# Decoder trunk on one core: TensorE warmed ahead of x's statistics, five weight units multiplied by TensorE, and half sums taken inside chunks 7, 9, 11 and 13

## The chip, the cores and the metric

One NeuronCore of a Trainium2 chip. The metric is the device time of one execution in microseconds (us). Engines: TensorE (PE in the profile; its weight loads are PEld), VectorE (DVE), ScalarE (ACT), GpSimd (POOL), and SyncE (SP), which issues the transfers.

## What is computed

Two layers over a sequence of 256 tokens of width 2048, float32. Each layer modulates a normalised x by a vector that comes from `c`:

```
c_act = silu(c)
for l in range(2):
    mod = c_act @ ada_w[l] + ada_b[l]                  # 2048 x 6144 weights for one row
    shift, scl, gate_res = split(mod, 3)
    h = rms(x, norm_g[l]) * (1 + scl) + shift
    z = h @ w_in[l]                                    # 2048 x 6144 (even layer)
    y = mixer branches and attention of z
    x = x + gate_res * ((y * silu(g)) @ w_out[l])
```

The change is in the opening: the statistics of x, `mod` of layer 0, h of layer 0, and the first twelve column slabs of `z`.

## The kernel before, in words

Everything is held transposed: a **chunk** is 128 of the 2048 features for all 256 tokens, so x and h are 16 chunks. `ada_w` is cut in **pieces** of 1024 columns; pieces 0 to 3 give scale and shift of h's chunks 0 to 3, 4 to 7, 8 to 11 and 12 to 15. A piece is 16 **units**: unit k holds 128 rows by 1024 columns (512 KB). Units are numbered on through the pieces: 0 to 15, 16 to 31, 32 to 47, 48 to 63.

*VectorE sums the units.* `add_units` (L1224) does acc += unit x cact[:, k] on 128 x 1024. In pieces 2 and 3 a unit holds two row blocks of half of the columns, and `half_units` (L1241, L1244) adds them by two instructions of 128 x 512, with a wait between. So the first eight units of such a piece finish its first half, which is enough for two chunks of h. `ada_done` counts the units added.

*TensorE sums over the partitions.* `reduce_part` (L929) multiplies 128 columns of acc by a column of ones; four of them make half of a piece. The trace shows two passes (rows of x1) for each float32 matmul. `half_sum` and `mod_sum` tell VectorE that the halves are there; `first_half(p)` and `second_half(p)` then add the bias (L1248), make the gain (L1261) and scale two chunks of x each (`norm_x`, L1297). ScalarE adds the shift (`full_h`, L523) and rounds a copy (L526), which releases the chunk for TensorE by `h_done`.

*Twelve slabs at once.* `unsplit_chunk(c)` (L895) multiplies chunk c of h by the 12 weight tiles of that chunk, 128 x 128 by 128 x 256 in plain float32, into six banks. The 192 weight tiles come in 12 transfers of 16 tiles (1 MB each, `load_wide`, L287), numbers 0 to 11. Only after chunk 15 are the banks read (ScalarE, L653), and the kernel goes on to slab 12 and the rest.

*x's statistics.* ScalarE squares the chunks of x (L517) into two buffers in turn; TensorE sums each by `x_stat` (L908), two matmuls with a moving operand of one column. VectorE makes the root and a diagonal of it (L1274 to L1288), `spread_token` (L919) spreads it, and ScalarE copies it (L645). `keep_warm` (L825) multiplies ones by the identity, 128 columns, for no result.

*The order around the change* is written out by hand on every engine. TensorE: 16 statistics, spread; 4 warm-up matmuls behind each of units 10 to 14; both halves of piece 0's sum; chunks 0 to 3; 12 warm-up matmuls; piece 1's sums; chunks 4, 5, 6; first half of piece 2; chunks 7, 8; second half of piece 2; chunks 9, 10; first half of piece 3; chunks 11, 12, 13; second half of piece 3 (L1087 to L1089); 6 warm-up matmuls; chunks 14, 15. SyncE issues all loads in one order: units and wide tiles mixed. A ring of 12 buffers holds the units, so the load of unit n waits until unit n - 12 is added, and wide load i waits until wide load i - 4 is used. A load that waits holds up all loads behind it.

Of the kernel before, what the change touches and what calls it, by code (L numbers as in the profile page):

```python
# [54 lines left out]

UNSPLIT = WIDE[0]
RING = 12
TILES = KC

def wide_done(i):
# [45 lines left out]
def build(nc, xT, params, pool_w, w_slabs, ada_units, x1_dram, outT):  # L107
    ctx = ExitStack()
    with ctx:
# [3 lines left out]
        def sem(name):  # L113
            return ctx.enter_context(nc.semaphore(name))
# [67 lines left out]
        acc_zero = sem("acc_zero")  # L182
        mod_sum = sem("mod_sum")
        half_sum = sem("half_sum")
        mod_done = sem("mod_done")
        cexp = sem("cexp")
        const = sem("const")
# [52 lines left out]
        def unit_slot(n):  # L240

            return n % RING if n < FIRST else n % 4

# [69 lines left out]
        @block.sync  # L313
        def _(sp):
            sp.sem_inc(lo_done, 4 + 2 * UNSPLIT)
            sp.sem_inc(ada_done, 4)
            sp.dma_start(par[:], params).then_inc(par_in, 16)
            def load_units(n, count, t):
                for u in range(count):
                    unit = n + u if t is None else n + u + 4 * t  # L320
                    if n >= FIRST:
                        sp.wait_ge(ada_done, unit + 1)
                    elif unit >= RING:
                        sp.wait_ge(ada_done, unit - RING + 5)
                    sp.dma_start(unit_at(n + u), ada_units[bass.ds(unit, 1)].rearrange("a p n -> p (a n)"))\
                      .then_inc(ada_in[unit_slot(n + u)], 16)

            def load_halves(p, first, last):
                for n in range(first, last):
                    unit, half, u = UNITS * p + n, n // 8, n % 8  # L330
                    sp.wait_ge(ada_done, unit - RING + 5)
                    sp.dma_start(unit_at(unit).rearrange("p (a n) -> p a n", a=2),
                                 ada_units[UNITS * p + 2 * u:UNITS * p + 2 * u + 2, :,
                                           PIECE // 2 * half:PIECE // 2 * (half + 1)]
                                 .rearrange("a p n -> p a n")).then_inc(ada_in[unit_slot(unit)], 16)

            load_units(0, 4, None)
            for part in range(2):
                sp.dma_start(X[:, HC * part:HC * (part + 1), :], xT[:, HC * part:HC * (part + 1), :])\
                  .then_inc(x_in[part], 16)  # L340
            load_units(4, UNITS - 4, None)
            load_wide(sp, 0)
            load_units(UNITS, 3, None)
            load_wide(sp, 1)
            load_units(UNITS + 3, 4, None)
            load_wide(sp, 2)
            load_units(UNITS + 7, 9, None)
            load_wide(sp, 3)
            for i, first, last in ((4, 0, 3), (5, 3, 8), (6, 8, 11), (7, 11, 13), (8, 13, 16)):
                load_halves(2, first, last)  # L350
                load_wide(sp, i)
            for i, first, last in ((9, 0, 8), (10, 8, 12), (11, 12, 16)):
                load_units(3 * UNITS + first, last - first, None)
                load_wide(sp, i)

            def step(w, t):
                load_slab(sp, w + AHEAD, t)
                load_units(*units_at(w), t)

            for w0, w1 in ((10, 14), (14, 22), (22, 34), (34, 48), (48, 62), (62, 72),  # L360
                           (72, 91), (91, 99), (99, 110), (110, 125), (125, 131),
                           (131, 132), (132, N_SLABS - AHEAD)):
                if w0 in (10, 34, 48, 62, 110, 131):
                    for w in range(w0, w1):
                        step(w, None)
                else:
                    run(sp, w0, w1, step)

            for j in range(KC - 4, KC):
                w = O1 + j  # L370
                sp.wait_ge(z_free[w % 2], w // 2 + 2)
                sp.dma_start(outT[:, j:j + 1, :], X[:, j:j + 1, :]).then_inc(last_store, 16)
            sp.wait_ge(last_store, 4 * 16)
# [443 lines left out]
        def _(pe):  # L817
# [67 lines left out]
                    if k == 7:  # L885
                        last.then_inc(pe_half, 1)

            def unsplit_chunk(c):

                pe.wait_ge(h_done, c + 1)  # L890
                for s in range(WIDE[0]):
                    i, k = (WIDE[0] * c + s) // TILES, (WIDE[0] * c + s) % TILES
                    if s == 0 or k == 0:
                        pe.wait_ge(wide_in[i % 4], 16 * (i // 4 + 1))
                    last = mm(wide(s), wide_tiles(i)[:, k, :], X[:, c, :], start=(c == 0 and s % 2 == 0),  # L895
                              stop=(c == KC - 1), skip_group_check=True)
                    if k % 8 == 7:
                        last.then_inc(pe_half, 1)
# [13 lines left out]
            def x_stat(i, runtime=None):  # L912
                pe.wait_ge(sq_done, (i if runtime is None else runtime) + 1)
                by_token(M, T[:, i % 2, :], i % KC == 0, i % KC == KC - 1).then_inc(stat_done, 1)
# [132 lines left out]

            pe.wait_ge(const, 3)
            for i in range(KC):  # L1050
                x_stat(i)
            spread_token(0)

            def warm_until(units, last):
                for u in range(units, last + 1):
                    pe.wait_ge(ada_done, u + 4)
                    keep_warm(4, O[:, SEQ:SEQ + P])

            halved = (2, 3)  # L1060

            def reduce_half(p, half):
                pe.wait_ge(ada_done, UNITS * p + 8 * (half + 1) + 4 if p in halved else UNITS * (p + 1) + 4)
                if not half and p:
                    pe.wait_ge(mod_done, p)
                for j in range(4 * half, 4 * half + 4):
                    ins = reduce_part(p, j, half=True)
                if not half:
                    ins.then_inc(half_sum, 1)

            for c in range(12):
                p = c // GROUP
                if c % GROUP == 0 and p not in halved:
                    if p:
                        warm_until(UNITS + 13, UNITS + 15)
                    else:
                        warm_until(11, 15)
                    reduce_half(p, 0)
                    reduce_half(p, 1)
                if c % GROUP == GROUP - 1 and p + 1 in halved:  # L1080
                    reduce_half(p + 1, 0)
                if c % GROUP == 1 and p in halved:
                    reduce_half(p, 1)
                unsplit_chunk(c)
            unsplit_chunk(12)
            unsplit_chunk(13)
            pe.wait_ge(ada_done, UNITS * 4 + 4)  # L1087
            for j in range(4, HC):
                reduce_part(3, j)  # L1089
            keep_warm(6, M[:, 0:P])  # L1090
            unsplit_chunk(14)
            unsplit_chunk(15)

# [106 lines left out]
        def _(dve):  # L1200
# [16 lines left out]
            def add_units(first, count, t):  # L1217
                for u in range(count):
                    unit = first + u if t is None else first + u + 4 * t
                    p = first // UNITS  # L1220
                    k = unit - UNITS * p
                    dve.wait_ge(ada_in[unit_slot(first + u)], 16 * unit_uses(first + u, t))
                    dve.wait_ge(ada_done, unit + 4)
                    dve.scalar_tensor_tensor(acc[:, p % 2, :], unit_at(first + u), cact[:, bass.ds(k, 1)],  # L1224
                                             acc[:, p % 2, :], ALU.mult, ALU.add).then_inc(ada_done, 1)

# [242 lines left out]
                norm_x(0, GROUP * p + 3)  # L1469

            dve.wait_ge(acc_zero, 1)
            add_units(0, 11, None)
            dve.wait_ge(stat_done, KC)
            rsqrt(0, QT, M[:, 0:QT], D_MODEL)
            token_diag()
            add_units(11, 5, None)
            dve.wait_ge(r_copied, 1)
            first_half(0)
            second_half(0)
            dve.wait_ge(acc_zero, 2)  # L1480
            add_units(UNITS, 16, None)
            dve.wait_ge(acc_zero, 3)
            first_half(1)
            second_half(1)
            half_units(2 * UNITS, 8)
            half_units(2 * UNITS + 8, 1)
            first_half(2)
            half_units(2 * UNITS + 9, 7)
            dve.wait_ge(acc_zero, 4)
            half_units(48, 1)  # L1490
            second_half(2)
            half_units(49, 7)
            half_units(56, 1)
            for j in range(6):
                lower_h(0, j)
            first_half(3)
            half_units(57, 7)
            second_half(3)
            for j in range(6, 14):
                lower_h(0, j)  # L1500
            lower_h(0, 14)
            lower_h(0, 15)

            def plain(w, t):
# [305 lines left out]
```

## Time and profile before

| | us |
|---|---|
| median of 3 runs | 976.7 (976.35 to 978.91) |
| the profiled execution, its own time | 974.86 |
| its span in the profile | 973.1 |
| TensorE busy | 943.4 (97%) |
| VectorE busy | 821.9 (84%) |
| ScalarE busy | 422.2 (43%) |

The profiled execution is 1.84 us under the median. "Busy" is the time in which an engine ran an instruction; the chain is followed back from the last instruction of the program to what released each step. All times of the trace are from the start of the span.

### The profile page before, as it was taken

How to read it: one execution, taken by the hardware profiler on the slowest of the kernel's cores; microseconds unless marked ns; L12 is line 12 of the kernel's file. 1: busy time of each engine (PE TensorE's matmuls, PEld its weight loads, DVE VectorE, ACT ScalarE, POOL GpSimd, SP SyncE). 2: the span in 40 equal slices, each digit the busy share in tenths (PEclk: the TensorE clock that was granted, in tenths of full speed). 3: DMA queues.
4: the chain of work that ended last, by engine and by line, in shares of the span. 5: the costliest groups of instructions: out<-in, count | busy, mean ns of one | idle time of the engine just before them, and what ended most of it. 6: DMA issues, size and time to landing. Idle time of an engine off the chain costs nothing.

```text
span 973.1 us, 18608 instructions
## 1 busy us (share of the span) xinstructions
PE 943.4 (97%) x7082; PEld 909.2 (93%) x7082; DVE 821.9 (84%) x1260; ACT 422.2 (43%) x726; POOL 65.1 (7%) x76
## 2 busy tenths in 40 slices
PE   4899999999999999999999999999999999999998
PEld 4887889999998999999999999999999989998887
DVE  5888979978998888998787999888999986879963
ACT  3110135445655444344444544444556555743331
POOL 1000000010110000222100000000011100000000
PEclk9999999999999999999999999999999999999999
DMA  9999988998876879899758555544455545688962
GB/s 366 412 403 403 413 320 277 323 348 326 327 266 242 314 262 337 326 364 355 284 198 319 179 190 180 178 143 151 153 184 185 175 168 199 201 313 295 358 224 78
DMA packets 76084, 261.28 MB, mean 269 GB/s; under 512 B 7776, under 2 KB 8416, under 8 KB 74096
## 3 DMA queue, kind: packets, MB, share of 16 engines
q1 hardware_dynamic: 73680, 251.38, 72.2%
q0 software_dynamic: 2336, 8.98, 2.5%
q8 instruction: 44, 0.72, 0.3%
q14 instruction: 24, 0.20, 0.1%
HBM read 256.07 MB, written 4.19 MB: 267 GB/s over the span
## 4 chain that ended last, share of the span: by engine, by line
PE 73%; DVE 18%; DMA 3%; issue 2%; ACT 2%; SPq 0%; DVEq 0%; ACTq 0%
PE bank L838 13%; PE bank L839 13%; PE bank L840 13%; PE bank L859 6%; DVE wlo L1214 6%; PE bank L895 5%; PE bank L982 4%; PE bank L984 4%; PE bank L985 4%; PE bank L857 3%; DMA ada<-ada_units 3%; DVE Y L1441 3%; DVE acc L1224 2%; PE bank L908 2%; DVE acc L1244 1%
## 5 line engine op out<-in xcount | busy, mean ns | idle before, releaser
L505 ACT ACTIVATE whi<-raw 128x1024 fp32r<-128x1024 f32 x258 | 272.1, 1060 | 384.5 <-PE bank L840 214.2
L1214 DVE TENSOR_TENSOR wlo<-raw,whi 128x1024 fp32r<-128x1024 f32 x258 | 312.6, 1227 | 71.9 <-ACT whi L505 70.7
L838 PE MATMUL bank<-hhi,whi 128*128 128x256 f32 x912 | 262.5, 288 | 3.1 <-DVE wlo L1214 1.4
L839 PE MATMUL bank<-hlo,whi 128*128 128x256 f32 x912 | 258.0, 283 | 0.0
L840 PE MATMUL bank<-hhi,wlo 128*128 128x256 f32 x912 | 257.9, 283 | 0.0
L1224 DVE SCALAR_TENSOR_TENSOR acc<-ada,cact,acc 128x1024 f32<-128x1024 f32 x140 | 183.0, 1307 | 22.9 <-DMA ada<-ada_units 12.6
L838 PEld LDWEIGHTS bank<-hhi,whi 128*128 128x128 f32 x912 | 174.8, 192 | 5.9 <-issue 3.1
L839 PEld LDWEIGHTS bank<-hlo,whi 128*128 128x128 f32 x912 | 174.9, 192 | 0.1
L840 PEld LDWEIGHTS bank<-hhi,wlo 128*128 128x128 f32 x912 | 174.8, 192 | 0.0
L982 PE MATMUL bank<-whi,hhi 128*128 128x256 f32 x512 | 146.7, 286 | 0.0
L984 PE MATMUL bank<-whi,hlo 128*128 128x256 f32 x512 | 144.8, 283 | 0.0
L985 PE MATMUL bank<-wlo,hhi 128*128 128x256 f32 x512 | 144.8, 283 | 0.0
L982 PEld LDWEIGHTS bank<-whi,hhi 128*128 128x128 f32 x512 | 98.2, 192 | 0.8 <-issue 0.7
L1441 DVE SCALAR_TENSOR_TENSOR Y<-U,par,Y 128x256 f32<-128x256 f32 x240 | 98.6, 479 | 0.0
L984 PEld LDWEIGHTS bank<-whi,hlo 128*128 128x128 f32 x512 | 98.2, 192 | 0.1
L985 PEld LDWEIGHTS bank<-wlo,hhi 128*128 128x128 f32 x512 | 98.2, 192 | 0.0
L859 PE MATMUL bank<-both_g,whi 128*128 128x512 f32 x256 | 89.7, 398 | 0.0
L838 PE MATMUL bank<-both_g,whi 128*128 128x256 f32 x256 | 73.2, 286 | 0.3 <-DVE both_g L1335 0.3
L839 PE MATMUL bank<-both_g,whi 128*128 128x256 f32 x256 | 72.4, 283 | 0.0
L840 PE MATMUL bank<-both_g,wlo 128*128 128x256 f32 x256 | 72.4, 283 | 0.0
L857 PE MATMUL bank<-both_g,wlo 128*128 128x256 f32 x240 | 68.1, 284 | 0.0
L859 PEld LDWEIGHTS bank<-both_g,whi 128*128 128x128 f32 x256 | 47.3, 188 | 10.4 <-DVE X L1350 0.2
(194 smaller groups left out, 1276.5 us busy)
## 6 DMA issues: line engine op xcount, KB each, us to landing
raw<-w_slabs SPq DMA_DIRECT2D x258, 512.0 KB, 4.6
ada<-ada_units SPq DMA_DIRECT2D x152, 512.0 KB, 6.6
pre<-ada_units SPq DMA_DIRECT2D x40, 512.0 KB, 15.5
raw<-w_slabs SPq DMA_DIRECT2D x6, 1024.0 KB, 15.9
V<-w_slabs SPq DMA_DIRECT2D x3, 1024.0 KB, 14.8
Y<-w_slabs SPq DMA_DIRECT2D x3, 1024.0 KB, 15.9
X<-xT SPq DMA_DIRECT2D x2, 1024.0 KB, 9.7
x_dram<-X POOLq DMA_DIRECT2D x4, 512.0 KB, 8.2
```

The source lines that it names most:

```text
L505: act.activation(whi[:, slot], raw[:, slot], ACT.Copy).then_inc(hi_done, 1)
L838: mm(out, whi[:, s, k, :], ahi[:, c, :], start=(c == 0), stop=False)
L839: mm(out, whi[:, s, k, :], alo[:, c, :], start=False, stop=False)
L840: last = mm(out, wlo[:, s, k, :], ahi[:, c, :], start=False, stop=(c == KC - 1))
L857: mm(out[:, 0:SEQ], wlo[:, s, k, :], ghi[:, c, :], start=False, stop=False, skip_group_check=True)
L859: last = mm(out[:], whi[:, s, k, :], flat(both_g[:, c]), start=(c == 0), stop=(c == KC - 1), skip_group_check=True)
L982: mm(out, hhi[:, c, tokens], upper, start=(c == 0 and q == 0), stop=False, skip_group_check=True)
L984: mm(out, hlo[:, c, tokens], upper, start=False, stop=False, skip_group_check=True)
L985: last = mm(out, hhi[:, c, tokens], lower, start=False, stop=(c == KC - 1), skip_group_check=True)
L1214: dve.tensor_tensor(wlo[:, s], raw[:, s], whi[:, s].bitcast(F32), ALU.subtract)\
L1224: dve.scalar_tensor_tensor(acc[:, p % 2, :], unit_at(first + u), cact[:, bass.ds(k, 1)], acc[:, p % 2, :], ALU.mult, ALU.add).then_inc(ada ...
L1441: ins = dve.scalar_tensor_tensor(Y[:, j, :], U[:, j, k:k + SEQ], par[:, wcol:wcol + 1], Y[:, j, :], ALU.mult, ALU.add)
```

## The change

1. TensorE starts with 30 warm-up matmuls, ahead of the statistics, and does 8 more between the statistics and the spread. The warm-ups behind units 10 to 14, ahead of piece 1's sum and behind the last half sum are gone; 3 stand behind the sums of pieces 0 and 1, after the first scaled chunk.
2. Units 9, 11, 13, 15 and 31 are multiplied by TensorE itself (`add_unit`): eight matmuls each with the unit as weights and one column of `cact` as moving operand, into the same banks as the sums. VectorE adds the other 27 of pieces 0 and 1. Piece 0's and 1's sums are taken by `reduce_whole`, which adds to what `add_unit` left. VectorE makes the statistics' root behind its first 8 units instead of behind 11.
3. The half sums of pieces 2 and 3 stand inside chunks 7, 9, 11 (ahead of the eighth tile) and 13 (ahead of the tenth). On VectorE `first_half(2)` comes two units later, and the six `lower_h` ahead of `first_half(3)` go to the end.
4. SyncE waits for `pe_added` where the buffer was used by one of the five units.

```diff
+ON_PE = (9, 11, 13, 15, 31)
+def added(unit):
+    return unit if unit >= UNITS else sum(u not in ON_PE for u in range(unit))
...
+            def slot_free(unit):
+                last = unit - RING
+                if last in ON_PE:
+                    sp.wait_ge(pe_added, ON_PE.index(last) + 1)
+                elif last >= 0:
+                    sp.wait_ge(ada_done, added(last) + 5)
...
+            def add_unit(unit):
+                p, k = unit // UNITS, unit % UNITS
+                pe.wait_ge(ada_in[unit_slot(unit)], 16 * unit_uses(unit, None))
+                first = not any(UNITS * p <= u < unit for u in ON_PE)
+                for j in range(HC):
+                    ins = mm(sums(p, j)[:, j:j + 1], unit_at(unit)[:, j * P:(j + 1) * P], cact[:, k:k + 1],
+                             start=first and j % (HC // 2) == 0, stop=False, skip_group_check=True)
+                ins.then_inc(pe_added, 1)
+
+            def reduce_whole(p):
+                units = [u for u in ON_PE if u // UNITS == p]
+                pe.wait_ge(ada_done, UNITS * (p + 1) - len(units) + 4)
+                for j in range(HC):
+                    ins = mm(sums(p, j)[:, j:j + 1], acc[:, p % 2, j * P:(j + 1) * P], ones[:, 0:1],
+                             start=False, stop=True, skip_group_check=True)
...
+                    if j == HC // 2 - 1:
+                        ins.then_inc(half_sum, 1)
+                ins.then_inc(mod_sum, 1)
+                pe.wait_ge(xr_done, GROUP * p + 1)
+                keep_warm(3, O[:, SEQ:SEQ + P])
...
+            keep_warm(30, O[:, SEQ:SEQ + P])
+            for i in range(KC):
+                x_stat(i)
+            keep_warm(8, O[:, SEQ:SEQ + P])
+            spread_token(0)
+            for unit in (9, 11, 13, 15):
+                add_unit(unit)
+            reduce_whole(0)
+            for c in range(4):
                 unsplit_chunk(c)
+            pe.wait_ge(mod_done, 1)
+            add_unit(31)
+            reduce_whole(1)
+            unsplit_chunk(4)
+            unsplit_chunk(5)
+            unsplit_chunk(6)
+            unsplit_chunk(7, 7, lambda: reduce_half(2, 0))
+            unsplit_chunk(8)
+            unsplit_chunk(9, 7, lambda: reduce_half(2, 1))
+            unsplit_chunk(10)
+            unsplit_chunk(11, 7, lambda: reduce_half(3, 0))
             unsplit_chunk(12)
-            unsplit_chunk(13)
-            pe.wait_ge(ada_done, UNITS * 4 + 4)
-            for j in range(4, HC):
-                reduce_part(3, j)
-            keep_warm(6, M[:, 0:P])
+            unsplit_chunk(13, 9, lambda: reduce_half(3, 1))
...
-            add_units(0, 11, None)
+            add_units(0, 8, None)
...
-            half_units(2 * UNITS, 8)
-            half_units(2 * UNITS + 8, 1)
+            half_units(32, 8)
+            half_units(40, 3)
             first_half(2)
-            half_units(2 * UNITS + 9, 7)
+            half_units(43, 5)
...
             half_units(56, 1)
-            for j in range(6):
-                lower_h(0, j)
             first_half(3)
             half_units(57, 7)
             second_half(3)
-            for j in range(6, 14):
+            for j in range(KC):
                 lower_h(0, j)
-            lower_h(0, 14)
-            lower_h(0, 15)
```

The changed file has other line numbers: L839 there is the warm-up, L924 the statistics, L935 the spread, L1071 `add_unit`, L1079 `reduce_whole`, L945 the half sums, L911 the chunks.

TensorE's first instructions, before (128x1 is a moving operand of one column; `raw`, `V` and `Y` are homes of wide tiles):

```order
L908 MATMUL bank<-ones,T 128x1 x32
L919 MATMUL bank<-KD,ones 128x128 x2
L825 MATMUL bank<-ident,ones 128x128 x20
L929 MATMUL bank<-ones,acc 128x1 x8
L895 MATMUL bank<-X,raw 128x256 x32
L895 MATMUL bank<-X,V 128x256 x16
L825 MATMUL bank<-ident,ones 128x128 x12
```

The same stretch of TensorE in the change (`pre` and `ada` hold the units):

```order
L839 MATMUL bank<-ident,ones 128x128 x30
L924 MATMUL bank<-ones,T 128x1 x32
L839 MATMUL bank<-ident,ones 128x128 x8
L935 MATMUL bank<-KD,ones 128x128 x2
L1071 MATMUL bank<-cact,pre 128x1 x16
L1071 MATMUL bank<-cact,ada 128x1 x16
L1079 MATMUL bank<-ones,acc 128x1 x8
L839 MATMUL bank<-ident,ones 128x128 x3
L911 MATMUL bank<-X,raw 128x256 x32
```

Between the spread and chunk 0 stood 20 matmuls of 128 columns and 8 of one column; now 40 of one column and 3 of 128.

TensorE at the end of the opening, before, from the first half sum of piece 3 on:

```order
L929 MATMUL bank<-ones,acc 128x1 x4
L895 MATMUL bank<-X,raw 128x256 x28
L895 MATMUL bank<-X,V 128x256 x8
L929 MATMUL bank<-ones,acc 128x1 x4
L825 MATMUL bank<-ident,ones 128x128 x6
L895 MATMUL bank<-X,V 128x256 x8
L895 MATMUL bank<-X,Y 128x256 x16
```

The same place in the change:

```order
L945 MATMUL bank<-ones,acc 128x1 x4
L911 MATMUL bank<-X,raw 128x256 x21
L911 MATMUL bank<-X,V 128x256 x5
L945 MATMUL bank<-ones,acc 128x1 x4
L911 MATMUL bank<-X,V 128x256 x11
L911 MATMUL bank<-X,Y 128x256 x16
```

The last half sum stands three tiles ahead of chunk 14 (27 tiles follow it instead of 24), and no warm-up follows it.

## Rows read from the trace of the kernel before

**Rows 1.** The page, its parts 1, 2 and 5: busy us; DMA share by slice; costly groups.

```profile
PE 943.4 (97%) x7082; PEld 909.2 (93%) x7082; DVE 821.9 (84%) x1260; ACT 422.2 (43%) x726; POOL 65.1 (7%) x76
DMA  9999988998876879899758555544455545688962
...
L1224 DVE SCALAR_TENSOR_TENSOR acc<-ada,cact,acc 128x1024 f32<-128x1024 f32 x140 | 183.0, 1307 | 22.9 <-DMA ada<-ada_units 12.6
```

**Rows 2.** Chain that ended last, opening: start us, us, what.

```profile
12.54 13.79 PE bank L908 x64
...
35.13 0.81 PE bank L929 x8
...
37.51 22.67 PE bank L895 x96
60.19 2.68 PE bank L825 x24
...
111.75 15.65 PE bank L895 x72
127.40 0.80 PE bank L929 x8
...
129.70 10.64 PE bank L895 x48
140.41 0.67 ACT U L653 x2
```

**Rows 3.** Unit 48's transfer in that chain: issue us, us to landing.

```profile
82.33 14.21 DMA ada<-ada_units
```

**Rows 4.** SyncE's issue of unit 15, then median us to landing (last number).

```profile
14.89 1.05 SPq L325 DMA_DIRECT2D ada<-ada_units  x1
...
ada<-ada_units SPq DMA_DIRECT2D x1, 512.0 KB, 14.9
```

**Rows 5.** The same for unit 31.

```profile
43.89 0.43 SPq L325 DMA_DIRECT2D pre<-ada_units  x1
...
pre<-ada_units SPq DMA_DIRECT2D x1, 512.0 KB, 14.8
```

**Rows 6.** VectorE's timeline: start us, us, idle before and its releaser.

```profile
83.55 0.16 DVE L1248 TENSOR_TENSOR mod<-bank,par 128x4 f32<-128x4 f32 x1 [2.74 <-PE bank L929]
...
98.07 0.15 DVE L1248 TENSOR_TENSOR mod<-bank,par 128x4 f32<-128x4 f32 x1
...
112.20 2.10 DVE L1305 TENSOR_TENSOR hlo<-X,hhi 128x256 fp32r<-128x256 f32 x6
114.22 0.15 DVE L1248 TENSOR_TENSOR mod<-bank,par 128x4 f32<-128x4 f32 x1
...
115.40 0.75 DVE L1241 SCALAR_TENSOR_TENSOR acc<-pre,cact,acc 128x512 f32<-128x512 f32 x1
...
126.04 0.75 DVE L1244 SCALAR_TENSOR_TENSOR acc<-ada,cact,acc 128x512 f32<-128x512 f32 x1
```

**Rows 7.** TensorE by stretch: us, PE busy (passes), granted clock, DMA share, GB/s.

```profile
12.54:26.32 13.78, 13.78 (x64) 1.00 1.02 412
28.11:32.00 3.89, 3.89 (x18) 1.00 1.02 417
475.90:478.90 3.00, 3.00 (x30) 1.00 1.02 418
479.30:482.70 3.40, 3.40 (x19) 0.52 0.90 369
...
38.90:42.20 3.30, 3.30 (x9) 0.50 1.03 411
...
66.20:69.50 3.30, 3.30 (x9) 0.50 1.05 388
```

**Rows 8.** GpSimd's timeline: the identity, which TensorE's start waits for.

```profile
3.14 0.29 POOL L390 TENSOR_SCALAR_AFFINE_SELECT ident<-ident 128x128 f32<-128x128 f32 x1 [0.25 <-POOL ident L389]
```

**Rows 9.** TensorE's timeline: start of chunk 4.

```profile
65.23 4.98 PE L895 MATMUL bank<-X,Y 128*128 128x256 f32 x14 [0.69 <-ACT X L523]
```

More of the change, by code:

```diff
@@ L184, in build @@
         half_sum = sem("half_sum")
+        pe_added = sem("pe_added")
         mod_done = sem("mod_done")
@@ L322, in load_units @@
                         sp.wait_ge(ada_done, unit + 1)
-                    elif unit >= RING:
-                        sp.wait_ge(ada_done, unit - RING + 5)
+                    else:
+                        slot_free(unit)
                     sp.dma_start(unit_at(n + u), ada_units[bass.ds(unit, 1)].rearrange("a p n -> p (a n)"))\
@@ L330, in load_halves @@
                     unit, half, u = UNITS * p + n, n // 8, n % 8
-                    sp.wait_ge(ada_done, unit - RING + 5)
+                    slot_free(unit)
                     sp.dma_start(unit_at(unit).rearrange("p (a n) -> p a n", a=2),
@@ L886, in wide_chunk, with unsplit_chunk @@
                         last.then_inc(pe_half, 1)
-            def unsplit_chunk(c):
+            def unsplit_chunk(c, at=None, between=None):
                 pe.wait_ge(h_done, c + 1)
                 for s in range(WIDE[0]):
+                    if s == at:
+                        between()
                     i, k = (WIDE[0] * c + s) // TILES, (WIDE[0] * c + s) % TILES
@@ L1049, in _ @@
             pe.wait_ge(const, 3)
[L1050 to L1060, printed above, removed]
+            def add_unit(unit):
[12 more added lines that the diff above has]
+                             start=False, stop=True, skip_group_check=True)
+                    if j == 0:
+                        ins.then_inc(ada_done, len(units))
+                    if j == HC // 2 - 1:
[3 more added lines that the diff above has]
+                keep_warm(3, O[:, SEQ:SEQ + P])
             def reduce_half(p, half):
-                pe.wait_ge(ada_done, UNITS * p + 8 * (half + 1) + 4 if p in halved else UNITS * (p + 1) + 4)
-                if not half and p:
+                pe.wait_ge(ada_done, UNITS * p + 8 * (half + 1) + 4)
+                if not half:
                     pe.wait_ge(mod_done, p)
@@ L1069, in reduce_half @@
                     ins.then_inc(half_sum, 1)
[L1071 to L1083, printed above, removed]
-                unsplit_chunk(c)
-            unsplit_chunk(12)
-            unsplit_chunk(13)
-            pe.wait_ge(ada_done, UNITS * 4 + 4)
-            for j in range(4, HC):
-                reduce_part(3, j)
-            keep_warm(6, M[:, 0:P])
+            keep_warm(30, O[:, SEQ:SEQ + P])
[7 more added lines that the diff above has]
+            for c in range(4):
+                unsplit_chunk(c)
+            pe.wait_ge(mod_done, 1)
[9 more added lines that the diff above has]
+            unsplit_chunk(11, 7, lambda: reduce_half(3, 0))
+            unsplit_chunk(12)
+            unsplit_chunk(13, 9, lambda: reduce_half(3, 1))
             unsplit_chunk(14)
@@ L1222, in add_units @@
                     dve.wait_ge(ada_in[unit_slot(first + u)], 16 * unit_uses(first + u, t))
-                    dve.wait_ge(ada_done, unit + 4)
+                    dve.wait_ge(ada_done, (unit if t is not None else added(unit)) + 4)
                     dve.scalar_tensor_tensor(acc[:, p % 2, :], unit_at(first + u), cact[:, bass.ds(k, 1)],
@@ L1475, in _ @@
             token_diag()
-            add_units(11, 5, None)
+            for unit in range(8, UNITS):
+                if unit not in ON_PE:
+                    add_units(unit, 1, None)
             dve.wait_ge(r_copied, 1)
@@ L1480, in _ @@
             dve.wait_ge(acc_zero, 2)
-            add_units(UNITS, 16, None)
+            add_units(UNITS, 15, None)
             dve.wait_ge(acc_zero, 3)
```

## The prediction

> **What bounds it now.** I read the page first. TensorE is busy for 97% of the span, so what the opening gives up or gains is passed on nearly whole to the end; the transfer engines are full in the first five slices, 122 us [rows 1]. The chain of waits comes next. Up to 140.41, where the banks of the twelve slabs are read, it goes by TensorE's statistics, warm-up, sum and chunks, then by a transfer that lands at 82.33 + 14.21 = 96.5, VectorE's adds, chunks 11 to 13, the last half sum, and chunks 14 and 15 [rows 2, 3]. Three things can set the opening's end, and I followed each.
>
> *Transfers* land one behind the other at about 410 GB/s, as fast as the engines go: unit 15 at 14.89 + 14.9 = 29.8 [rows 4], unit 31 at 43.89 + 14.8 = 58.7 [rows 5], unit 48 at 96.5 [rows 3]. No edit moves these as long as SyncE stays ahead. It is ahead by 14 to 15 us.
>
> *VectorE* takes from 98.07 to 126.04 + 0.75 = 126.79 for units 49 to 63 and what stands between them, 28.7 us; the last seven take 126.79 - 115.40 = 11.4, or 1.63 each, and six `lower_h` fill 114.22 - 112.20 = 2.0 [rows 6]. TensorE, busy with chunk 13, takes up the last sum 0.6 us after them [rows 2].
>
> *TensorE* has two speeds. Before 26.3 the 64 statistics passes take 13.78 / 64 = 0.215 us each. Passes of 128 columns also begin at that price (18 passes in 3.89 us) and then, 3.9 us after the engine resumed, cost half (0.112, from 24 in 2.68) [rows 7, 2]. One-column passes do cost half at the full clock: eight in 0.80 [rows 2], 30 records in 3.00 from 475.9 on [rows 7]; with the steps between matmuls I take 0.109. But 3.4 us after those began, at 479.3, the granted clock falls to the level of 0.50, which is 1.2 GHz against 2.4 [rows 7]. The column reads 1.00 in the statistics too, so there I go by the pass. The 64 passes ran without a gap and never left the slow price. A chunk's pass costs 15.65 / 72 = 0.217, so a tile 0.434 [rows 2].
>
> **The change, part by part, up to chunk 0.** *30 warm-ups.* They start at 3.4, when the identity is there [rows 8]. With 3.9 us at 0.215 (18 passes), then 42 x 0.112 = 4.7, they end at 12.0, just as x comes (statistics started at 12.54 before). Cost nothing; were all 60 passes slow, 12.9 us, the start would be 16.3, 3.8 late.
>
 That gains 2.6. VectorE's root needs 28.11 - 26.32 = 1.8 [rows 7], until 25.5, beside the next item.
>
> *Eight warm-ups and the spread*: 16 + 4 passes at 0.215 = 4.3, until 28.0. The clock has risen by then (27.6).
>
> *Four units and the sum on TensorE*: 64 + 16 one-column passes. This is the term that decides. All fast: 80 x 0.109 = 8.7. All slow: 17.2. I take what both stretches of such passes show: fast for 3.4 us (31 passes, until 31.4), then 33 x 0.215 = 7.1 for the units (38.5), 1.7 for the first half sum (40.2), 1.7 for the second (41.9). VectorE and ScalarE need 37.51 - 35.94 = 1.6 from the first half sum to the chunk, hidden; the three warm-ups are 6 x 0.215 = 1.3. **Chunk 0 starts at 43.2 instead of 37.5.** The units themselves are not the limit: unit 15 lands at 29.8, TensorE gets to it after 35. What VectorE is spared (4 x 1.3 [rows 1]) buys nothing, since it waits for this sum.
>
> The Trainium skill says otherwise ("TensorE: Matmul & The Clock Gate", part 1): the throttled state is the default, sustained activity lifts it, and idleness brings it back, so passes without gaps should keep the clock. By that the statistics before would have turned fast, and the trace disagrees: 64 in a row, none fast. By the Trainium skill's rule the 80 passes would cost 8.7 instead of 13.9; that is rival A.
>
> *SyncE.* A load waits for the unit twelve before it. Unit 21's now waits for TensorE's unit 9, some 5 us later than today; unit 31's waits for VectorE's unit 19, which follows `second_half(0)` (41.9 + 1.3) by 4 x 1.3, so it goes out at about 48.4 instead of 43.9 [rows 5] and has 10 us left until its turn at 58.7. The queue covers this: nothing. Without that cover each us of delay there would be one at the transfers.
>
> **From chunk 0 to the end.** Chunks 0 to 3 took 22.67 with one slow stretch in them [rows 2]; again: 65.9. Unit 31 (landed long since) 16 x 0.109 = 1.7; the half sum 0.9 (68.5); from there 1.6 as above, and the second half sum and the three warm-ups end at the same time: chunk 4 at 70.1 instead of 65.23 [rows 9]. The 12 warm-ups ahead (2.68) are gone and paid with.
>
> To the eighth tile of chunk 7: 43 tiles x 0.434 = 18.6, and 1.7 for a slow stretch behind the one-column passes, as 38.9 to 42.2 and 66.2 to 69.5 had [rows 7]: 90.4, half sum until 91.2. VectorE today waits there 2.74 and starts at 83.55 [rows 6]. Now it has finished unit 42 at 89.1 and waits 2.1. Then 1.2 for `first_half(2)`, 5 x 1.64, unit 48's 1.64: 102.3, where it stood at 98.07 although the transfer allows 98.1. TensorE's second half sum, 24 tiles on, is done at 102.5. From there today's 28.7 less the 2.0 of `lower_h` [rows 6]: unit 63 at **129.2** instead of 126.8. TensorE stands ready in chunk 13 (with one wait in chunk 11, for unit 55), sums in 0.85 with no 0.6 of delay, 129.70 - 128.20 = 1.5 to chunk 14, where the three tiles left of chunk 13 and not the six warm-ups cover, and 10.64 as today [rows 2]: **142.2 instead of 140.4, 1.8 later.** `lower_h` costs its 2.0 behind chunk 14; TensorE's 10.6 us there cover it, and the high and low parts of slab 12 wait for ScalarE behind 140.4 anyway.
>
> Sum: +5.7 (chunk 0), -0.8 (chunk 4 less late, as the warm-ups go), -0.5 (chunk 4 to unit 48: part of VectorE's wait goes), -2.0 (`lower_h`), -0.6 (last sum at once) = +1.8. On the execution's 974.9 that is 976.7; the median is 1.84 above that execution, so I predict **978.5** against 976.7.
>
> **Rivals.** *A, the clock holds* through one-column passes once it is up. For: the warm-ups are new in front of them. Against: the fall at 479.3. (The Trainium skill's rule above speaks for this rival.) Statistics end at 20.0, spread 23.4, unit 15 from its landing to 31.5, sum, chunk 0 at 34.1, chunk 4 at 63.0 (unit 31 lands at 58.7). The transfer of unit 48 then rules: 98.1 + 26.7 = 124.8, + 0.9 + 1.5 + 10.6 = 137.8: 2.6 less, 974.1; with the slow stretches of chunks 0 and 4 spared as slack, down to 973. This is the case in which the faster side lies.
>
> *B, the eight warm-ups do not lift the clock.* They and the spread are 4.3 us long, the rise at 32.0 took 3.9 [rows 7]; a little more and the 80 passes are all slow: 28.0 + 17.2 + 1.3 = 46.5, 3.3 more. It decides by one number: with chunk 0 at 43.2 the sum is +1.8, and it moves us for us, so the kernel is slower from chunk 0 at about 41.4 on. 46.5 gives +5.1, **981.8**.
>
> *C, the delay is swallowed.* If the statistics stay fast for longer (end near 21) chunk 0 comes at 40.5 to 41.5 and the gates at unit 48 and 63 even it out: 976 to 977. The half sums inside the chunks do then all they can.
>
> **How the numbers follow.** About 0.3% (2.9 us) is what a measurement of this kernel can tell from no change. My forecast, 977 to 980.5, has 0.45; C 0.17; B 0.20; A 0.18. A falls two thirds on the faster side (its 973 to 974 lies at that bound of 973.8), and I add a little for gains that I do not see: faster 0.15. Slower takes B and a third of the forecast: 0.35. The rest, 0.50, is within 0.3%. The range runs from A's better end to a little past B: 973.2 to 982.5.
>
> **What would show it.** Right: one-column passes of L924 at about 0.11 us for some 3 us and then at 0.215; the same turn within L1071; chunk 0 at 42 to 44; chunk 4 near 70; VectorE waiting ahead of `first_half(2)` with unit 48 done near 102; no L1305 ahead of the last units; the banks read near 142. Wrong: chunk 0 ahead of 38 (A), L1071 slow from its first pass (B), or landings later than 96.5 for unit 48, which would mean that SyncE ran dry.

## The result, and the profile after

| | before | after |
|---|---|---|
| median | 976.7 us | 981.3 us of 4 runs (977.97 to 982.60) |
| the profiled execution, its own time | 974.9 | 978.0 |
| its span | 973.1 | 976.2 |
| the banks of the twelve slabs read | 140.4 | 145.1 |
| from there to the end of the span | 832.7 | 831.1 |

The change is slower: 981.26 / 976.71 = 1.0046, 95% interval [1.0024, 1.0067], or 4.5 us. It is a small difference, but the interval is clear of 1. The forecast was 978.5 and +1.8.

The page of the change, its parts 1 and 2 (as rows 1, with the granted clock of TensorE in 40 slices):

```profile
PE 959.4 (98%) x7174; PEld 925.2 (95%) x7174; DVE 816.4 (84%) x1255; ACT 422.6 (43%) x726; POOL 63.7 (7%) x76
...
PEclk8699999999999999999999999999999999999999
DMA  9999978898886888899858655544555445688962
```

TensorE is busy for 16 us more, all of it in the opening. The 30 warm-ups at the start take 9.9 us and the five units 12.0, against the older warm-ups that went. The first two slices, 49 us, show the clock at 8 and 6 tenths, and at a lower clock the same pass is a longer busy one. The transfers are as full as before.

The chain that ended last, over the opening (answers to rows 2 and 9; start us, us, what):

```profile
3.48 9.89 PE bank L839 x60
...
16.45 8.69 PE bank L924 x40
25.14 3.62 PE bank L839 x16
...
29.61 10.34 PE bank L1071 x64
39.96 3.41 PE bank L1079 x16
...
44.86 21.93 PE bank L911 x96
...
71.46 20.12 PE bank L911 x86
...
102.84 0.80 PE bank L945 x8
...
104.93 0.67 DVE acc L1271
...
130.41 1.05 PE bank L945 x8
131.47 13.60 PE bank L911 x54
145.13 0.67 ACT U L667 x2
```

From 3.48 to the second half sum of piece 2, at 102.84, nearly all is TensorE's own work; between the first statistics stand ScalarE's squares. Then come VectorE's adds of units 49 to 63, and from 130.41 on TensorE again. Chunk 0 starts at 44.86 instead of 37.51. The lateness is then made up in part: chunk 4 at 71.46 (6.2 late), the last half sum at 130.41 (127.40 before, 3.0 late). At the end of the opening the lateness is 4.7 again: the 54 passes behind the last half sum take 13.60 us where 54 at the price of rows 2, 0.217, take 11.7.

TensorE's windows say when the clock stood where (window, us, busy us and instructions, granted clock, DMA share, GB/s; answers to rows 7):

```profile
8.00:9.00 1.00, 1.00 (x7) 1.00 1.09 442
9.00:10.00 1.00, 1.00 (x8) 1.00 1.02 430
...
16.00:17.00 1.00, 0.94 (x7) 0.73 1.01 410
17.00:18.00 1.00, 1.00 (x7) 0.50 1.05 422
...
29.00:30.00 1.00, 1.00 (x7) 0.50 0.99 410
30.00:31.00 1.00, 1.00 (x10) 0.94 1.01 418
...
33.00:34.00 1.00, 1.00 (x9) 0.77 1.00 401
...
47.00:48.00 1.00, 1.00 (x5) 0.91 1.04 414
```

The warm-ups end at 13.37. They ran at half speed (7 records touch 1 us) until 9.6, 6.1 us after their first, and at full speed from then on (12 touch each us), though the clock's column reads 1.00 from the start. The one-column statistics begin at the full clock and lose it at 16.5. The eight warm-ups and the spread begin at 25.1 and the clock is back at 30.1; the units' one-column passes lose it at 33.5; three warm-ups, from 43.4 on, and chunk 0 bring it back at 47.2. In each of these two stretches of one-column passes it went down, and it came back 5.0 and 3.8 us after the first warm-up behind them.

VectorE (start us, us, idle before it and releaser; answers to rows 6):

```profile
41.77 0.16 DVE L1278 TENSOR_TENSOR mod<-bank,par 128x4 f32<-128x4 f32 x1 [9.53 <-PE bank L1079]
...
92.41 0.16 DVE L1278 TENSOR_TENSOR mod<-bank,par 128x4 f32<-128x4 f32 x1 [2.62 <-PE bank L945]
...
103.66 0.16 DVE L1278 TENSOR_TENSOR mod<-bank,par 128x4 f32<-128x4 f32 x1 [0.29 <-PE bank L945]
...
129.61 0.75 DVE L1274 SCALAR_TENSOR_TENSOR acc<-ada,cact,acc 128x512 f32<-128x512 f32 x1
```

The four units taken from VectorE turn into a wait of 9.53 us for TensorE's sum. Unit 48 is done at 103.4 (98.1 before), unit 63 at 130.36 (126.8). SyncE did not run dry: unit 31 went out at 50.06 and landed 8.7 later, at 58.8, where it landed before [rows 5], and unit 48 at 87.25 (answers to rows 3: the issue, and the time to landing in the last column):

```profile
87.25 0.43 SPq L339 DMA_DIRECT2D ada<-ada_units  x1
...
ada<-ada_units SPq DMA_DIRECT2D x1, 512.0 KB, 9.6
```

That is 96.9 for unit 48, against 96.5 [rows 3].

Behind the opening the profiled execution got 1.6 us back (831.1 against 832.7). One wait of 1.4 us of TensorE for VectorE between 500 and 600 is there before and not after. Over this and all runs below, the rest lies between 831.1 and 835.4, in no order that goes with a part of the change; the second profile of the change has 832.4 and is 5.2 us longer than the one before.

### The profile page after: what moved, and what is told of

Its sections match the earlier page's. It is cut to its first block, busy times and chain, and to the rows that moved or that the text cites. A ratio compares the mean times of both kernels' runs of the same rounds, so it can differ in the third digit from the quotient of the medians.

```text
span 976.2 us, 18782 instructions
## 1 busy us (share of the span) xinstructions
PE 959.4 (98%) x7174; PEld 925.2 (95%) x7174; DVE 816.4 (84%) x1255; ACT 422.6 (43%) x726; POOL 63.7 (7%) x76
## 4 chain that ended last, share of the span: by engine, by line
PE 82%; DVE 14%; ACT 1%; issue 1%; DMA 1%; POOL 0%; DVEq 0%; SPq 0%; ACTq 0%; POOLq 0%
PE bank L852 13%; PE bank L853 13%; PE bank L854 13%; PE bank L911 7%; PE bank L873 6%; DVE wlo L1244 4%; PE bank L998 4%; PE bank L1000 4%; PE bank L1001 4%; PE bank L871 3%; DVE Y L1471 2%; PE bank L839 2%; PE bank L891 2%; PE bank L897 2%; PE bank L893 2%; PE bank L924 1%
## 5 line engine op out<-in xcount | busy, mean ns | idle before, releaser
L1254 DVE SCALAR_TENSOR_TENSOR acc<-ada,cact,acc 128x1024 f32<-128x1024 f32 x138 | 180.3, 1307 | 19.4 <-DMA ada<-ada_units 9.4
```

## The experiments

My theory: one-column passes lose the clock, so the opening as changed makes chunk 0 late and TensorE slow, while the half sums inside the chunks (part 3 of the change) gain. Rivals: the half sums cost something too; the eight warm-ups are what is lost; moving units to TensorE is wrong in itself, whatever the clock does. Per kernel, from its profiled execution: the start of chunk 0, the banks read, and the rest of the span; then the median of its runs and the ratio, with its interval, to runs of the kernel before on the same chip (their medians lie between 976.2 and 976.7).

| kernel | chunk 0 | banks | rest | median | ratio |
|---|---|---|---|---|---|
| before | 37.5 | 140.4 | 832.7 | 976.7 | |
| the change | 44.9 | 145.1 | 831.1 | 981.3 | 1.0046 [1.0024, 1.0067] |
| the change, again | 45.6 | 145.9 | 832.4 | 980.1 (one) | |
| half sums alone | 38.7 | 139.1 | 832.6 | 973.4 | 0.9964 [0.9947, 0.9980] |
| half sums alone, again | 39.3 | 138.7 | 832.8 | 974.4 | 0.9981 [0.9968, 0.9993] |
| opening alone | 44.9 | 147.1 | 831.5 | 983.0 | 1.0061 [1.0042, 1.0079] |
| the change, 128 columns | 35.9 | 139.8 | 832.7 | 974.3 | 0.9973 [0.9958, 0.9988] |
| before, 128-column statistics | 36.5 | 142.7 | 833.3 | 976.1 | 0.9993 [0.9978, 1.0009] |
| the change without the eight | 46.1 | 146.8 | 831.8 | 980.6 | 1.0048 [1.0032, 1.0064] |
| half sums and warm-ups | 37.0 | 139.0 | 831.3 | 973.4 | 0.9973 [0.9957, 0.9988] |
| half sums, two late units | 39.1 | 139.0 | 835.4 | 975.1 | 0.9985 [0.9974, 0.9996] |
| the same, again | 38.5 | 139.4 | 834.0 | 973.9 | 0.9970 [0.9960, 0.9980] |
| the change, wide statistics | 39.7 | 140.2 | 833.0 | 974.5 | 0.9983 [0.9971, 0.9995] |
| the change, wide units | 39.8 | 139.0 | 832.8 | 973.6 | 0.9968 [0.9957, 0.9979] |

**The two parts apart.** To the kernel before, part 3 of the change alone:

```diff
+            unsplit_chunk(7, 7, lambda: reduce_half(2, 0))
...
+            unsplit_chunk(9, 7, lambda: reduce_half(2, 1))
...
+            unsplit_chunk(11, 7, lambda: reduce_half(3, 0))
...
+            unsplit_chunk(13, 9, lambda: reduce_half(3, 1))
...
-            keep_warm(6, M[:, 0:P])
```

> The kernel before with part 3 of the change alone: half sums inside chunks 7, 9, 11, 13, first_half(2) two units later, lower_h at the end. Theory (the opening's one-column passes cost the time, part 3 saves some): chunk 0 stays at 37.5, VectorE ends unit 63 2.0 us earlier (124.8), the banks are read near 138, and the kernel is 2.5 to 3 us faster than before. Rival (the half sums inside the chunks themselves delay the chunks): same as before or slower, the banks read at 140 or later.

And the change with the half sums and VectorE's order put back as before:

> The change without its part 3: warm-ups, units on TensorE, but half sums and lower_h where they stood before. Theory: this part costs what part 3 hides, so 6 to 7 us slower than before, chunk 0 at 43 to 48. Rival (part 3 does the harm): about as fast as before, within 1 us.

Both times are as expected: -3.0 us and +6.6. Half sums alone reach the banks 1.3 us ahead of the kernel before (139.1, where I had expected 138) though x landed late in that execution and chunk 0 began 1.2 later. The opening alone reaches them 6.7 later:

```profile
44.85 22.65 PE bank L911 x96
...
134.06 0.80 PE bank L945 x8
136.35 10.64 PE bank L911 x48
```

So the change is the sum of a part that gains and one that loses more. The half sums inside the chunks cost less than they save, and that rival is out.

**Wider moving operands.** The change with 128 columns in place of one in the statistics, the units' passes and the sums of pieces 0 to 3. The same weights are loaded and as many passes run; every column of the result is the same, and VectorE reads one of them.

```diff
-                    ins = mm(sums(p, j)[:, j:j + 1], unit_at(unit)[:, j * P:(j + 1) * P], cact[:, k:k + 1],
+                    ins = mm(spot(p, j), unit_at(unit)[:, j * P:(j + 1) * P], cact[:, k:k + 1].broadcast_to([P, P]),
...
-                x_stat(i)
+                x_stat_wide(i)
```

> The change with 128 columns instead of one in the moving operand of every statistic, added unit and sum of pieces 0 to 3 (each result then stands in 128 equal columns); same number of passes. Theory (the clock falls behind one-column passes): it stays up through the whole opening, a pass costs 0.11 instead of 0.215, chunk 0 starts near 34, the banks are read near 138, 3 to 4 us faster than before, 8 faster than the change. Rival (TensorE is late because of the number of its passes, or of its weights): nothing moves, chunk 0 at 44.

It is 7.0 us faster than the change. Up to chunk 0 the windows never leave the full clock (TensorE, the stretch in which the change stood mostly at 0.50). Later, from 60.2 to 63.6, it fell once, behind a wait of 2.46 us for unit 31, although every pass there had 128 columns:

```profile
28.00:30.00 2.00, 2.00 (x21) 1.00 1.05 426
...
34.00:36.00 2.00, 1.85 (x15) 1.00 1.03 412
...
59.03 2.71 PE L1086 MATMUL bank<-cact,pre 128*128 128x128 f32 x16 [2.46 <-DMA pre<-ada_units]
...
60.00:62.00 2.00, 2.00 (x13) 0.55 1.03 385
```

Statistics take 9.76 us in place of 11.77 in the change and 13.78 before, and chunk 0 begins at 35.9 (I had expected 34). Yet it is no faster than the half sums alone: the gain was 2.1 us, not the 3 to 4 that I expected. The lead at chunk 0 ends at unit 31, whose transfer lands at 58.9 (58.7 before [rows 5]) and for which TensorE now waits. Behind that, its chain goes by unit 48's transfer:

```profile
83.91 14.21 DMA ada<-ada_units
...
139.79 0.67 ACT U L671 x2
```

It landed at 98.1 (96.5 before [rows 3]), and the banks are read at 139.8. So chunk 0 ahead of the half sums' 38.7 had nothing left to give here. It also settles the third rival: five units on TensorE, with wide passes, cost no more than leaving them on VectorE, and gain nothing either.

**The kernel before with 128-column statistics** (the same edit to `x_stat` alone):

> The kernel before with 128 columns in the statistics' moving operand, nothing else. Theory: the clock rises within the statistics, they end at 22 to 23 instead of 26.3; chunk 0 comes at most 1 us earlier since VectorE's units rule then, and the end stays: 0, within 1 us. Rival (the start of the program is slow whatever the passes do): statistics still 13.8 us.

```profile
12.58 11.09 PE L919 MATMUL bank<-ones,T 128*128 128x128 f32 x64 [12.58 <-ACT T L517]
```

The 64 passes take 11.09 us in place of 13.78: without a warm-up ahead of them they brought the clock up, which the one-column ones never did. The time is the same, as expected, since the units' transfers and VectorE stand behind it (its profiled execution has a slow stretch in chunks 11 to 13, 17.12 us for 72 passes against 15.65 [rows 2], which the median doesn't show).

**The eight warm-ups.** The change without the line `keep_warm(8, O[:, SEQ:SEQ + P])`:

> The change without the eight warm-ups between statistics and spread. Theory (they lift the clock in some executions only, for 3.4 us, which gives back 1.7 us and costs 3.4): the 80 one-column passes are all slow, 17.2 us, and start about 2 us earlier; the time is that of the change within 1.5 us, with less spread between runs. Rival (they keep the clock up for the whole of the added units): 5 us slower than the change.

The same time as the change. From 24 to 48 the clock never rises:

```profile
24.00:48.00 24.00, 22.20 (x99) 0.50 1.02 413
```

The eight take 3.62 us, but without them TensorE waited 1.79 us at that place for VectorE's root, so from the last statistic to the end of the spread they cost 1.5 us (4.47 against 3.01). They give the units' passes 3.4 us at the full clock, by which these passes and the sum took 13.76 us and not 16.85. In the profiles the eight thus bring chunk 0 some 1.6 us forward (44.9 against 46.1, though the statistics began 0.4 us earlier without them), and not the 1.7 gained for 3.4 lost of my expectation; in the medians no difference shows (+4.3 us without them, +4.5 with them). They are not what is lost.

**Warm-ups with the units on VectorE.** Half sums alone, with 30 warm-ups ahead of the statistics and 8 ahead of the spread:

> The kernel of e1 with part 1 of the change as well: 30 warm-ups ahead of the statistics, 8 ahead of the spread, units all on VectorE as before. Theory: statistics end 1 to 2 us earlier, but the eight slow warm-ups (3.4) fill that, and unit 48's transfer rules the end: same as e1 within 0.5 us; so the opening's loss is in the units on TensorE. Rival (the warm-ups ahead do the harm): 2 us or more slower than e1.

As expected, the half sums' time: the warm-ups cost nothing where VectorE's units hold chunk 0 back anyway, and bring nothing.

**Which one-column passes.** Two kernels split the edit of the 128 columns: statistics only, and units and sums only.

> The change with one edit: the sixteen statistics matmuls of x (64 passes) use a moving operand of 128 columns in place of one; the five units' 80 passes stay at one column. In the run with 128 columns everywhere the statistics took 9.8 us at full clock and the whole was 7.0 us faster than the change. Theory (the narrow passes lose the clock, wherever they stand): statistics end near 23.5, at full clock, so warmings until the spread are fast too; then the units' narrow passes start fast and lose the clock after about 3.5 to 6 us; 80 passes cost 3.5 to 6 us of fast ones and the rest at 0.21 each, some 12 to 14 us, chunk 0 at 41 to 43.5, the whole 1 to 4 us faster than the change (977 to 980). Rival (the statistics alone are to blame, a stretch that begins at full clock holds it): chunk 0 before 38, the whole within 1 us of the run with 128 columns everywhere (974 to 975).

> The change with the other half of that edit: the units' 80 passes, the adds and the half sums of pieces 0 to 3 use 128 columns, the statistics stay at one column. Theory: statistics as in the change, ending near 25; the 80 wide passes start slow and the clock comes back after some 4 to 6 us of them and then stays, so they take 12 to 13 us less half of that: 10.5 to 12 us in place of 13.8, chunk 0 at 41 to 43, fast from its first pass, the whole 3 to 5 us faster than the change (976 to 978). Rival (width does not matter for the units): within 1 us of the change (980 to 982.5).

Both came out faster than my theory had it, 974.5 and 973.6. The first time is the rival's (974 to 975), so the clock has to tell the two apart. With wide statistics the units lose it as the theory has it; from TensorE's windows:

```profile
26.00:28.00 2.00, 2.00 (x20) 1.00 1.03 412
28.00:30.00 2.00, 2.00 (x14) 0.66 1.05 428
30.00:32.00 2.00, 2.00 (x11) 0.50 0.98 403
```

They start at full clock at 24.85 and lose it at 28.6, and chunk 0 starts at 39.67, 1.3 us ahead of the theory's 41 to 43.5 and behind the rival's 38. So the rival's mechanism, that a stretch which begins fast stays fast, is out, though its time came true. With wide units the clock comes back at 29.9 and stays until 111.8; chunk 0 starts at 39.77 (theory 41 to 43) and its 96 passes take 20.72 us (22.67 before):

```profile
29.51 7.40 PE bank L1079 x64
36.90 0.91 PE bank L1087 x8
...
39.77 20.72 PE bank L915 x96
```

Both expectations had chunk 0 some 1.3 us too late. What failed in them for the most part is the last step, from chunk 0 to the time. I had let each us of chunk 0 count; but at 39.7, two us behind the kernel before, next to nothing is lost at the banks (139.0, and 140.2 with a slow stretch behind the last half sum that comes up again below). All kernels with the half sums that start chunk 0 by 39.8 read the banks by 140.2; the kernel before (140.4) and the one with wide statistics (142.7) do without the half sums.

**What ends the opening once the clock is out of the way.** In the half sums alone TensorE still waited 2.20 and 1.74 us for VectorE in chunks 11 and 13. I took two units of piece 3 (52 and 58) from VectorE and put them on TensorE inside chunks 11 and 12:

```diff
+            unsplit_chunk(11, 2, lambda: add_late(LATE[0]), {7: lambda: reduce_half(3, 0)})
+            unsplit_chunk(12, 2, lambda: add_late(LATE[1]))
```

> The kernel of e1 (half sums alone) with units 52 and 58, whose time on VectorE sets the end of the opening, multiplied by TensorE inside chunks 11 and 12, between dense chunks. Theory (behind unit 48's transfer VectorE's adds set the end, and a short run of one-column passes inside chunks does not lower the clock): VectorE is spared 2 x 1.63, limited by unit 63's transfer to about 1.9, so 1 to 2 us faster than e1, 4 to 5 faster than before. Rival (any unit on TensorE costs what it does in the change): slower than e1 by 1 us or more.

I had expected 1 to 2 us less than the half sums alone, and measured 1.7 more. The waits of TensorE for VectorE in chunks 11 and 13 are gone, and the short runs of one-column passes inside chunks 11 and 12 (16 passes in 1.68 us each) left the clock up, as expected. But the banks are read at the same point. The chain of waits:

```profile
114.39 12.39 DMA raw<-w_slabs
...
126.80 1.06 ACT whi L507
127.85 0.41 ACT X L525
...
139.02 0.67 ACT U L655 x2
```

A slab's transfer lands at 126.8. ScalarE's high part of it (`whi`) stands ahead of the shift for chunk 14 (L525) on ScalarE, and so chunk 14 waits for that transfer (TensorE stands still for 1.3 us). I ran this kernel and the half sums alone again on one chip:

> The kernel with half sums and two late units on TensorE once more, beside the half sums alone on the same chip. Both showed the banks of chunks 8 to 15 read at the same point (139.0 and 139.1), and what followed took 835.4 and 832.6 us in the two profiled executions. Theory (the slab whose transfer landed at 126.8 sets the end of the opening, so freeing TensorE and VectorE gives nothing): banks read at 139 again. What follows: if its transfers from 400 to 480 were late by chance, the rest is 831 to 833.5 this time and the timed medians of the two agree within 0.5 us; if the two units on TensorE change the phase of the transfers for good, the rest is again about 835 and the median 1 to 2 us above the half sums alone.

> The half sums alone once more, as the partner of the run with the two late units: banks read at 138.5 to 139.5, the rest 831 to 833.5, median 2.5 to 3.5 us below the kernel before (973 to 974).

Now 973.9 and 974.4, so the 1.7 us were not the units' doing; the rest of the span, 835.4 then and 834.0 now, is on the high side of the others both times, and whether it belongs to the two units stays open. The half sums alone had the same chain this time:

```profile
116.20 10.26 DMA raw<-w_slabs
...
138.70 0.67 ACT U L653 x2
```

By VectorE's adds (the first run's chain) and by this slab (the second's) the banks come at the same 139. Seven rows of the table, five kernels, have them between 138.7 and 139.8.

**The change once more**, for a second profile:

> The change once more, for a second profile. Theory: where the time is near 981 instead of 978, the clock does not rise during the eight warm-ups, or rises so that the units get less of it: chunk 0 starts at 46 to 48 instead of 44.9. Rival: chunk 0 at 45 and the time lost elsewhere.

Chunk 0 at 45.6; the clock rose at 30.8 and fell at 34.3, as in the first profile, so this theory is out. Of the 2.1 us by which this execution is longer (980.1 against 978.0), 0.7 are there at chunk 0, since x landed later and the statistics began at 13.84 instead of 13.21, and 1.4 come behind the banks. The last 54 passes took 13.59 us again:

```profile
132.20 13.59 PE bank L911 x54
```

No version beats the half sums alone: 973.4 and 974.4, with 973.4 to 975.1 for those with wide passes, warm-ups or late units beside them. All are 1.2 to 3.0 us below the kernel before.

## Why the prediction was right in its direction and short in its size

The direction was right (+1.8 forecast, +4.5 measured), and 981.3 lies within the range. The outcome held likeliest, at 0.50, was a time within 0.3% of the kernel before; slower, which came, had 0.35. The time is nearly that of rival B, 981.8, but that is luck and not its mechanism: behind the eight warm-ups the clock did rise in both profiles, and without them it did not. Step by step:

- *30 warm-ups, nothing.* Mis-sized in the first profile. I took the slow part as 3.9 us, from one rise at 32.0 [rows 7]; it was 6.1, and they ended at 13.37, not 12.0, which began the statistics 0.8 us late. In the second profile the slow part was 3.5 us, they ended at 12.09, and x's landing set the start of the statistics, as forecast.
- *Statistics.* Right that they lose the clock (at 16.5; I had 15.9), and wrong by a little in the price at full clock: two in 1.11 us, 0.55 each and not 0.46. End 25.14, forecast 23.7; of the 1.4 between them 0.8 is the late start and 0.6 the price.
- *Eight warm-ups and the spread*, 4.3: measured 4.47. The clock rose at 30.1, not 27.6, and so fell later too.
- *Four units and the sum*, 13.9 us: measured 13.76, with 3.4 us of them at full clock, as forecast. The term that was to decide was right, and rival A is out: the clock did not hold. In the Trainium skill's "TensorE: Matmul & The Clock Gate", part 1, what counts is that TensorE is busy. The runs disagree for passes of one column: TensorE is busy without a gap in the change from 25.14 to 44.86 and loses the clock; in the kernel with wide units, the same passes in the same order with 128 columns keep it. 64 + 8 wide passes took 8.3 us where 64 + 8 narrow ones took some 12.
- *Chunk 4 at 70.1, unit 48 done at 102.3*: 71.5 and 103.4, late by 1.4 and 1.1, somewhat less than chunk 0 (1.7). SyncE stayed ahead, as forecast, and VectorE waited 2.62 (2.1).
- *The half sums, -2.6*: part 3 alone gave -3.0 and -2.2 timed in two runs. Right. In the change it gave less: the banks are read at 145.1 with it and 147.1 without, -1.9.
- *The end, unit 63 to the banks, 13.0 us.* This is the step that failed outright. Unit 63 was done at 130.4 (1.2 late, inherited); from there to the banks it took 145.13 - 130.36 = 14.8, 1.8 too many. I wrote "10.64 as today". But TensorE waited 1.74 us ahead of the last half sum, did eight one-column passes, and 1.0 us behind them the clock fell, from 132.5 to 135.9, which at half clock costs 1.7 us:

```profile
130.41 1.05 PE L945 MATMUL bank<-ones,acc 128*128 128x1 f32 x8 [1.74 <-DVE acc L1274]
...
132.00:133.00 1.00, 1.00 (x6) 0.76 0.98 324
133.00:134.00 1.00, 1.00 (x4) 0.50 1.01 377
...
135.00:136.00 1.00, 1.00 (x4) 0.53 0.89 365
```

Nothing stands between that place and the banks that could cover it. The prediction charged such a stretch to chunks 4 to 7, rightly (86 passes in 20.12 us; 18.65 + 1.7 forecast), and none to the end. Where the last half sum follows on work without a wait (before, the opening alone, and the change without the eight) the 48 passes of chunks 14 and 15 took 10.64 us. With a wait of 1.74 us and the narrow sum the clock fell in both profiles of the change and in the one with wide statistics, and held in the first profile of the half sums alone, where both are the same. Narrow passes are not needed for such a fall. In the change with wide units, whose sums have 128 columns too, it came at 111.8, behind 2.69 us of waiting for unit 55 (its chain, then TensorE's windows):

```profile
111.30 1.64 PE bank L950 x8
...
111.00:112.00 1.00, 0.70 (x5) 0.92 1.07 434
```

The change with 128 columns lost it at 60.2 in the same way (above), and kept it behind the same 1.74 us ahead of its wide last sum. In the half sums' second profile and the half sums with warm-ups it fell at 112.9 and 112.8, behind waits of 2.7 us, where TensorE had slack. So a wait of TensorE of 1.7 us and more stands ahead of each of these falls, and the width of the sum does not decide; which wait is followed by one stays open.

So the 2.9 us by which the banks miss the forecast of 142.2 are 1.2 inherited from the warm-ups and the statistics and 1.7 from the stretch at the end. The rest of the span gave 1.6 back, so the profiled execution, 978.0, is 1.3 above the 976.7 forecast for it. The timed difference is larger than that of the first pair of profiles (4.5 against 3.1); the second profile of the change shows 5.2, and nothing in the two tells why the timed runs lie nearer to it.

The sum by parts was: opening +4.4 forecast, +6.7 measured at the banks; half sums -2.6 forecast, -1.9 measured there. And the expectation, in rival A, that an earlier chunk 0 brings 2.6 us held only as far as the half sums bring them: chunk 0 at 35.9 was no faster than at 38.7. A's 137.8 at the banks took unit 48 to be there when it was before, and in that kernel it landed 1.6 us later.

## What to carry to other kernels

Moving work to an idle engine is priced by what that engine does next, not by its idle share: four units on TensorE freed 5.2 us of VectorE, which turned into a wait of 9.5 for TensorE, in large part because the passes were of a kind that costs TensorE its clock. Where a stretch of one-column float32 matmuls stands in front of real ones, try a wider moving operand: with 128 columns a pass cost nearly the same here, and the clock stayed up through the stretch. It does not help against the falls behind a wait. And before taking a wait away, follow the other chains that end at the same point; here VectorE's adds and a slab's transfer let the banks be read at the same 139, so taking away either of them alone brought nothing.

## What the runs showed of the hardware that I had not expected

- A float32 pass with a moving operand of 128 columns costs little more than one of one column at the full clock: 8 in 0.91 us in the wide sums against 8 in 0.80.
- The granted clock in the profile reads 1.00 from the start of the span, while the passes until 9.6 take twice as long as later ones; before its first change it can't be relied on, and the pass time has to be taken.
- Float32 passes with one column, back to back, did not bring the clock up (64 in 13.78 us), and lost it where they began at the full clock (at 16.5 and 33.5 in the change). With 128 columns the same passes brought it up (64 in 11.09 us) and kept it (64 in 7.40 us).
- From the first warm-up to the first fast pass it took between 3.5 and 6.1 us in the eight profiles that begin with 30 warm-ups, two of them of one kernel. For the second rise of the change, from the eight warm-ups on, it took 5.0 us in both its profiles. One such time, taken from one profile, is no price to forecast with.
- A wait of TensorE of 1.7 to 2.7 us could be followed by 3.4 us at half clock, or not: 1.74 us ahead of the last half sum was followed by it in the change and not in the half sums alone, and 2.20 us before chunk 11's sum in neither.
